# First block of a two-block network on Trainium2: key scores, expert choice, spread and expert sum joined into one stage per layer, with the scores of all experts kept in DRAM

## What is computed

```python
def block(hb):                                   # lax.map over blocks of 128 tokens
    q = (hb @ w_q).reshape(n, PEER_HEADS, 2, PEER_DK_HALF)          # 8 heads, 2 halves of 128
    s = jnp.einsum('nhpk,pek->nhpe', q, keys)                       # 128 keys a half
    v_top, i_top = lax.top_k(s, PEER_TOPK)                          # 16
    cand = (v_top[:, :, 0, :, None] + v_top[:, :, 1, None, :]).reshape(...)
    sc, pos = lax.top_k(cand, PEER_TOPK)
    e = i1 * N_KEYS + i2                                            # of 16384 experts
    g = jax.nn.softmax(sc.astype(jnp.float32), axis=-1)
    a = jax.nn.gelu(jnp.einsum('nhkd,nd->nhk', u_tab[e], hb)) * g
    return jnp.einsum('nhk,nhkd->nd', a, v_tab[e])
x = x + mod[5] * _peer(h, *peer_args)
```

## Time and profile before

| what | us |
|---|---|
| median of 3 runs | 5837.4 |
| lowest and highest | 5792.01 and 5842.43 |
| the profiled execution | 5842.43 |
| its span, first to last instruction | 5842.2 |

### The profile page before, as it was taken

One profiled execution on the slowest core, in us unless ns is written; L12 is line 12 of the kernel. 1 busy time (PEld: TensorE's weight loads), 2 busy tenths in 40 slices (PEclk: granted clock), 3 DMA queues, 4 the chain that ended last, 5 costly groups with the idle time before them and its releaser, 6 DMA issues. The chain is left out here.

```text
span 5842.2 us, 68094 instructions
## 1 busy us (share of the span) xinstructions
PE 4566.9 (78%) x24318; PEld 3796.7 (65%) x24318; DVE 3182.0 (54%) x4967; ACT 1507.1 (26%) x1871; POOL 1088.4 (19%) x304
## 2 busy tenths in 40 slices
PE   6747968766999999999447745999996666985678
PEld 1635735255888888888336635888886666974477
DVE  1533327895555555555354297888886343631455
ACT  0211212132222222222212213333333312531333
POOL 0300011264222221221210135333330010000000
PEclk9857989888999999999767868999998787995689
DMA  6202212334333333332213304555554103541154
GB/s 247 66 19 63 81 66 87 138 136 162 125 109 124 126 117 116 126 124 84 102 33 99 119 29 172 184 185 188 187 192 132 45 26 91 164 129 53 49 143 137
DMA packets 545188, 668.47 MB, mean 114 GB/s; under 512 B 15866, under 2 KB 467482, under 8 KB 543182
## 3 DMA queue, kind: packets, MB, share of 16 engines
q1 hardware_dynamic: 543236, 659.80, 33.7%
q10 hardware_dynamic: 1776, 6.34, 0.3%
HBM read 613.04 MB, written 53.05 MB: 114 GB/s over the span
## 5 line engine op out<-in xcount | busy, mean ns | idle before, releaser
L1320 POOL TENSOR_TENSOR ex_ulo<-ex_u,ex_uhi 128x2048 fp32r<-128x2048 f32 x128 | 595.2, 4650 | 1579.3 <-ACT ex_uhi L1354 1579.3
L119 PE MATMUL bank<-hThi_l,ex_uhi 128*128 128x512 f32 (+1 forms) x2048 | 690.1, 337 | 52.2 <-POOL ex_ulo L1320 52.2
L119 PE MATMUL bank<-hTlo_l,ex_uhi 128*128 128x512 f32 (+1 forms) x2048 | 689.8, 337 | 0.0
L119 PE MATMUL bank<-hThi_l,ex_ulo 128*128 128x512 f32 (+1 forms) x2048 | 689.7, 337 | 0.0
L119 PE MATMUL bank<-ex_vhi,ex_ahi 128*128 128x512 f32 x1536 | 607.6, 396 | 53.6 <-DVE peer_l L1394 50.8
L1394 DVE TENSOR_TENSOR peer_l<-peer_l,bank 128x512 f32<-128x512 f32 x756 | 496.9, 685 | 239.6 <-PE bank L119 239.6
L119 PE MATMUL bank<-ex_vlo,ex_ahi 128*128 128x512 f32 x1536 | 603.9, 393 | 0.0
L119 PE MATMUL bank<-ex_vhi,ex_alo 128*128 128x512 f32 x1536 | 603.7, 393 | 0.0
L1372 DVE TENSOR_TENSOR ex_vlo<-ex_v,ex_vhi 128x2048 fp32r<-128x2048 f32 x128 | 385.7, 3013 | 279.4 <-ACT ex_vhi L1360 279.4
L119 PEld LDWEIGHTS bank<-hThi_l,ex_uhi 128*128 128x128 f32 x2048 | 390.0, 190 | 95.4 <-POOL ex_ulo L1320 52.9
L119 PEld LDWEIGHTS bank<-hTlo_l,ex_uhi 128*128 128x128 f32 x2048 | 390.0, 190 | 42.6
(11 more groups left out here) (476 smaller groups left out, 9305.9 us busy)
## 6 DMA issues: line engine op xcount, KB each, us to landing
ex_u<-peer_u_in SPq DMA_DIRECT2D x128, 1024.0 KB, 8.3
ex_v<-peer_v_in SPq DMA_DIRECT2D x128, 1024.0 KB, 5.4
dense_weights<-sp_buf SPq DMA_DIRECT2D x12, 4096.0 KB
gu_w<-ffn_w_up_in SPq DMA_DIRECT2D x88, 512.0 KB, 5.2
mg_wg<-w_in_in SPq DMA_DIRECT2D x32, 1024.0 KB, 5.3
ex_g<-dense_weights SPq DMA_DIRECT2D x64, 512.0 KB, 4.5
ada_w<-w_ada_in SPq DMA_DIRECT2D x12, 2048.0 KB, 8.2
pc_ada_w<-w_ada_in SPq DMA_DIRECT2D x12, 2048.0 KB
```

Of the source, the lines that this page charges most:

```text
L119: ins = pe.matmul(psum, a, b, start=first and i == 0, stop=last and i == len(terms) - 1)
L1320: pool.tensor_tensor(u2[1][:, s, :, :], u[:, s, :, :], u2[0][:, s, :, :].bitcast(F32), ALU.subtract).then_inc(u_lo, 1)
```

## The change

The four stages become one, `peer`, of which all steps are written out (no hardware loop). It has two phases.

Score phase: 72 steps of the same form, 8 of query weights and 64 of u, n = 0 to 71. ACT splits the high half of step n+1 ahead of taking the results of n, POOL the low half of n+1 ahead of weighing the groups of n. The raw tile and its low half now lie in the same memory, so a tile's slot is free only when its products are done (`scored`, later `used`); there are three slots of tiles in layer 0 and four in layer 1 (`ring`), and three of high halves. The gelus of all experts are written to `act_s` (three slots) and stored by SP in DRAM (`expert_scores`). Beside these steps DVE does the choice of the first pair of tiles and then the second; PE turns the picks after u step 9 and 16 (layer 1: 14), then spreads two groups per step for 32 steps (layer 1: one group per step for 32 steps), and from u step 52 on the 12 chunks of the next modulation, one per step.

Value phase: 64 steps. SP loads the stored scores s and the dense weights g of step m (`fetch_weighted`), then v of step m+3 (m+4 in layer 1). DVE multiplies both experts' columns in one operation, splits v, and makes the low half of a after ACT's high half. PE's `combine(m)` adds all 64 steps into the eight PSUM banks (four in layer 1), so DVE's additions are gone, and at the end each bank is multiplied by the gate and added to x. u and the query weights are laid out on the host so that each partition's part of a tile is one run of 8 KB.

```diff
-def key_scores(K, l, hT, t0, top, topi):
...
-def expert_choice(K, l, top, topi, tiles, choice):
...
+def peer(K, l, hT, x, t0):
...
+    U = NEXP // width
+    first_v = PH + U
+    ring = 3 if tw > 256 else 4
+    slots = 3
+    G = 8
+    n_groups = tw // G
+    per_step = 2 if tw > 256 else 1
+    turn_at = [9, 16] if pairs == 2 else [14]
+    spread_from = turn_at[-1] + 1
+    spread_to = spread_from + n_groups // per_step
+    ada_from = spread_to + 3
+    n_ada = 6 * D // 512 if nxt else 0
...
+        raw = ExitStack()
+        wt = sb("w", [P, ring, KD, width], scope=raw)
+        raw.close()
+        w_lo = sb("wlo", [P, ring, KD, width], F32R)
+        w_hi = sb("whi", [P, slots, KD, width], F32R)
+        act_s = sb("s", [P, 3, 2, tw])
...
+            def _(sp):
+                def fetch(n):
+                    if n >= ring:
+                        if n - ring < first_v:
+                            sp.wait_ge(scored, 2 * (n - ring) + 2)
+                        else:
+                            sp.wait_ge(used, n - ring - first_v + 1)
+                    if n < PH:
+                        src = K.dram["peer_w_q"][l, n]
+                    elif n < first_v:
+                        src = K.dram["peer_u"][l, n - PH]
+                    else:
+                        m = n - first_v
+                        sp.dma_start(wt[:, n % ring, :, :].rearrange("p (e j) c -> p e (j c)", e=2),
+                                     K.dram["peer_v"][l][m * width:(m + 1) * width, :].rearrange("(e p) d -> p e d", p=P)).then_inc(w_in[n % ring], 16)
...
+                def keep_scores(m):
+                    sp.wait_ge(freed, 2 * (PH + m) + 2)
+                    sp.dma_start(K.scores[m, :, 0:2 * tw], act_s[:, m % 3, :, :].rearrange("p e t -> p (e t)")).then_inc(s_stored[m % 3], 16)
+
+                def keep_choice(b):
+                    sp.wait_ge(copied, 16 * (b + 1))
+                    sp.dma_start(K.dense[b], buf[:, b % 2, :, :].rearrange("p i t -> p (i t)")).then_inc(g_stored[b % 2], 16)
+
+                def fetch_weighted(m):
+                    if m >= 3:
+                        sp.wait_ge(mulled, m - 2)
+                    sp.dma_start(act_s[:, m % 3, :, :].rearrange("p e t -> p (e t)"), K.scores[m, :, 0:2 * tw]).then_inc(sg_in[m % 3], 16)
+                    sp.dma_start(gw[:, m % 3, :, :], K.dense[0:nb, :, m * 128:(m + 1) * 128].rearrange("b j n -> j b n")).then_inc(sg_in[m % 3], 16)
...
+                for n in range(1, first_v + lag - PH):
+                    if n < first_v + ring:
+                        fetch(n)
+                    m = n - lag
+                    if m < 0:
+                        continue
+                    keep_scores(m)
+                    for g in groups_after(m):
...
+                    sp.wait_ge(s_stored[s], 16 * ((U - s + 2) // 3))
+                if nxt:
+                    for s in range(2):
+                        sp.wait_ge(row_stored[s], 16 * (n_ada // 2))
+                for m in range(U):
+                    fetch_weighted(m)
+                    if first_v + m + ring < first_v + U:
+                        fetch(first_v + m + ring)
+                    if m == 4:
+                        for s in range(2):
+                            sp.dma_start(mod5[:, s, :], K.ada[l, s:s + 1, 5 * D:6 * D].broadcast_to([P, D])).then_inc(mod_in, 16)
...
+                def split_lo(n):
+                    s = n % slots
+                    pool.wait_ge(hi_ready, n + 1)
+                    pool.tensor_tensor(w_lo[:, n % ring, :, :], wt[:, n % ring, :, :], w_hi[:, s, :, :].bitcast(F32),
+                                       ALU.subtract).then_inc(lo_ready, 1)
...
+                split_lo(0)
+                for n in range(first_v):
+                    if n + 1 < first_v:
+                        split_lo(n + 1)
+                    for g in groups_after(n - PH):
+                        weigh(g)
...
+                def score(n):
+                    pe.wait_ge(lo_ready, n + 1)
+                    for j in range(2):
+                        i = 2 * n + j
+                        if i >= 4:
+                            pe.wait_ge(freed, i - 3)
...
+                        match_keys(n - 1)
+                    m = n - PH
+                    if m in turn_at:
+                        turn(turn_at.index(m))
+                    for g in groups_after(m):
+                        spread(g)
+                    if ada_after(m) is not None:
+                        ada(ada_after(m))
...
+                def combine(m):
...
+                    pe.wait_ge(v_lo, m + 1)
+                    pe.wait_ge(a_lo, m + 1)
+                    for o in range(outs):
...
+                            last.then_inc(outed, 1)
+                    if m < U - 1:
+                        last.then_inc(used, 1)
+
+                for m in range(U):
+                    combine(m)
...
+                def take_scores(m):
+                    for j in range(2):
+                        i = 2 * (PH + m) + j
+                        act.wait_ge(scored, i + 1)
+                        if m >= 3:
+                            act.wait_ge(s_stored[m % 3], 16 * (m // 3))
+                        act.activation(act_s[:, m % 3, j, :], K.ps[i % 4][:, 0:tw], ACT.Gelu_apprx_tanh).then_inc(freed, 1)
...
+                def split_a(m):
+                    act.wait_ge(mulled, m + 1)
+                    if m >= slots:
+                        act.wait_ge(used, m - slots + 1)
+                    act.activation(a2[0][:, m % slots, :, :], a[:, m % slots, :, :], ACT.Copy).then_inc(a_hi, 1)
...
+                for n in range(first_v):
+                    split_hi(n + 1)
...
+                        take_query(n)
+                    else:
+                        take_scores(m)
+                    if 1 <= n <= PH:
...
+                        take_spread(g)
+                    if ada_after(m) is not None:
+                        take_ada(ada_after(m))
+                split_a(0)
+                for m in range(1, U):
+                    split_hi(first_v + m)
+                    split_a(m)
...
-def spread_choice(K, l, choice, t0, tw):
...
-def experts(K, l, hT, acc, t0, tw):
...
+                def multiply(m):
+                    dve.wait_ge(sg_in[m % 3], 32 * (m // 3 + 1))
+                    if m >= slots:
+                        dve.wait_ge(a_hi, m - slots + 1)
+                    dve.tensor_tensor(a[:, m % slots, :, :].rearrange("p e (b t) -> p e b t", t=64),
+                                      act_s[:, m % 3, :, :].rearrange("p e (b t) -> p e b t", t=64),
+                                      gw[:, m % 3, :, :].rearrange("p b (e t) -> p e b t", t=64), ALU.mult).then_inc(mulled, 1)
...
+                for m in range(U):
+                    multiply(m)
+                    split_v(m)
+                    dve.wait_ge(a_hi, m + 1)
+                    dve.tensor_tensor(a2[1][:, m % slots, :, :], a[:, m % slots, :, :], a2[0][:, m % slots, :, :].bitcast(F32),
+                                      ALU.subtract).then_inc(a_lo, 1)
...
-            experts(K, l, hT, acc, t0, TALL - t0)
-            with stage(K, "step") as (block, step):
...
+        peer(K, l, hT, x, t0)
```

## The result

The changed kernel takes 7255.8 us, the median of 4 runs (7248.2 to 7257.5); the kernel before took 5839.9 beside it. The ratio is 1.243, with a 95% interval of 1.238 to 1.248: slower by 1416 us. The forecast was 7466, in a range of 7130 to 7850. Direction and mechanism came out as forecast; the rise, forecast as 7466 - 5837 = 1629 us, was put 213 us too high.

What follows compares the result with a forecast made beforehand. PE bounds the old expert loop; stages around it are not PE-bound. The profiled 5842.4 us plus 834.9 for layer 0 and 794.0 for layer 1 gave 7471, adjusted to the median as 7466 us; range 7130 to 7850.

Steps and rivals of the forecast that it cites:

- The step that decides: SP's value-phase queue: s and g wait behind v, leaving gaps of 13.6 us in layer 0, 10.9 in layer 1.
- The rows to look for: Value phase: g releases DVE, PE clock about 0.9 or below, v load waits for PE, sums every 27 and 19 us.
- Rival A: SP's value-phase queue: s and g arrive before the sum, so gaps and cold starts go; 5602 us, chance 0.04.
- B (full clock throughout): Value phase: PE keeps full clock through the gaps, 128 x 2.5 us less; 7146 us, chance 0.08.
- C (half clock throughout): Value phase: PE's bursts stay at half clock throughout, 603 us more; 8069 us, chance 0.09.
- the prediction's range: Whole kernel: own case 7200 to 7770 us, errors not all on one side; widened towards two rivals, 7130 to 7850.
- 63 gaps: Value phase, each layer: 64 bursts with 63 gaps; gaps total 856.8 us in layer 0, 686.7 in layer 1.
- The turn: Value phase, layer 0: products 10.88, cold start 2.5 and gap 13.6 us make a period of 27.0 us.
- The transfers: Layer 0's value-phase gap: v, s and g, 2 MB, take 8.3 us, bounds 6.95 to 9.6.
- Layer 0's score part: Layer 0, score phase 1058.5 us plus a handover of 15 to the value phase; 1073.5 us together.
- the wait for the choice: Layer 0's score phase: PE waits 8 us for DVE's choice, slowed by POOL's splits; bounds 0 and 36.
- Layer 1's loop: Layer 1's score phase: 32 spreading steps loop through ACT, POOL and PE, 12.3 us each, 393.6 us; bounds 7.9 and 14.5.

Runs made afterwards that it cites:

- experiment 1: Changed kernel with SP's loads of s and g issued three steps ahead, in front of the waiting v load; 5585.3 us, 0.958 of the kernel before.
- experiments 1 and 2: The second: changed kernel with s and g loaded three steps ahead and POOL weighing groups before splitting; 5478.8 us, 0.942 of the kernel before.
- Experiment 6: Changed kernel plus 44 useless PE products before each sum in layer 1's value phase; 7156.0 us.
- Experiment 7: Changed kernel with only POOL's score-phase order altered: it weighs the groups before splitting the next low part; 7140.0 us.
- experiment 5: Changed kernel plus 36 useless PE products before each sum in layer 1's value phase; 7221.3 us.
- experiment 3: Changed kernel with SP's loads of s and g issued one step ahead, before the v load that waits for the sum; 5870.5 us.
- in after: The changed kernel itself, as measured without any further edit; 7255.8 us.

## Why the prediction was right, and where its sizes were off

**The mechanism.** The step that decides, that the s and g of step m+1 stand behind a load of v that waits for sum m, is shown by experiment 1: the same work with another order loses the whole rise. The rows to look for came: DVE released by g, a clock of 0.75 and 0.69, SP's v load 0.03 us behind the sum, and a sum every 26 and 18 us (forecast 27 and 19). Rival A fell, because the three slots were there but never filled ahead. The rule of the Trainium skill's "DMA: Bandwidth & Descriptors", section "Rules for kernel authors", to issue early and wait late, is obeyed in full by experiments 1 and 2, and the trace agrees with it there (sums 10.88 us apart, clock 1.00). Three slots didn't make a transfer early whose issue stood behind the wait of another one (26.2 us per turn).

**Rivals B and C.** B (full clock throughout) fell with the rows at 2524.33, C (half clock throughout) with the return to 0.23 us between products inside every sum, after some 10 products of 48 in layer 0. Experiment 6 measures the clock's price at 1.9 us per sum in layer 1, and 10.4 products of 0.2 us make 2.1 in layer 0, where the forecast had 2.5 for both.

**Where 220 us of the two regions went**, in the prediction's terms. All of the larger errors lie on the same side, which the prediction's range had ruled out ("they will not all fall on one side"); it held the result all the same.

- *The number of gaps.* The term "63 gaps" was wrong. SP is held only while there is a v load to issue, and the last three (layer 1: four) steps have none. SP's and DVE's rows at the end of layer 0 show it; first SP, where the last v is followed by three pairs without a wait for PE:

```profile
3474.26 0.37 SPq L1058 DMA_DIRECT2D pr_w<-peer_v_in  x1
3474.68 0.47 SPq L1081 DMA_DIRECT2D pr_s<-expert_scores  x1
3475.19 0.43 SPq L1082 DMA_DIRECT2D pr_g<-dense_weights  x1
3475.67 1.62 SPq L1081 DMA_DIRECT2D pr_s<-expert_scores  x1
```

```profile
3482.21 1.23 DVE L1392 TENSOR_TENSOR pr_a<-pr_s,pr_g 128x1024 f32<-128x1024 f32 x1 [20.63 <-DMA pr_g<-dense_weights]
...
3486.69 1.22 DVE L1392 TENSOR_TENSOR pr_a<-pr_s,pr_g 128x1024 f32<-128x1024 f32 x1
```

  There were 61 gaps and 60. The missing two and three, with their cold starts, are 2 x 16.1 + 3 x 13.4 = 72 us. This is the one term that was wrong in kind; the others were missed in size. The order of SP's queue, read to its end, would have told it.
- *The turn.* Layer 0: 26.1 us in the mean against 27.0, over 61 turns 55. In the turn shown the transfers took 7.9 us (forecast 8.3), DVE's chain 4.7 (4.9), and tail and SP 0.2 (0.33: SP issued 0.03 us after the product's end and not 0.17); over the layer some 10.4 products per sum ran at half clock (12.5). Layer 1: 17.9 against 18.84, over 60 turns 55; about 9.5 products at half clock.
- *The transfers.* DMA issues of layer 0's value phase (KB each, median us to landing) are quicker than in the loop before, where v took 6.4. The engines' share is lower too, 0.24 against 0.35; that this is the reason wasn't tested:

```profile
pr_w<-peer_v_in SPq DMA_DIRECT2D x57, 1024.0 KB, 4.9
pr_s<-expert_scores SPq DMA_DIRECT2D x59, 512.0 KB, 5.8
pr_g<-dense_weights SPq DMA_DIRECT2D x59, 512.0 KB, 7.0
```

- *Layer 0's score part*, 23 us less: a step with two groups takes 14.6 us where 15.2 was taken (32 of them, 18 us), the wait for the choice, put at 8, didn't occur, and PE waited 12.2 us before the value phase instead of 15. Against that the twelve chunks of the modulation took 8 us more: they added 8.1 each instead of 7.9, and the first added 13.6, of which PE spent 3.9 waiting for its load.
- *Layer 1's loop*, 11.6 us against 12.3 (32 of them, 23 us). POOL's weighing took 1.90 us; the row used had 2.70, but there DVE's one-hots ran beside it. Experiment 7 shows both ends of it, 1.90 and 2.88. The part as a whole fell by 10 only, since the steps without a group took 7.2 us in the mean: 231 us for the 32, where 214.4 and 3 for the turn were taken. Some of them fall beside DVE's choice, where POOL's splits take up to 6.6 us and PE waits for them by up to 2.9.

The sum of the value parts, 186 of 220 us, is thus 72 for gaps that don't exist, 110 for turns taken too long, and 4 not assigned.

**The choice beside POOL's splits.** DVE's rows in layer 1's choice, and POOL's in the same time:

```profile
4152.32 4.52 DVE L1352 CAST pr_place<-pr_pos 128x256 f32<-128x256 uint32 x1
...
4158.99 8.70 DVE L1362 TENSOR_TENSOR pr_hot<-pr_half,iota 128x4096 f32<-128x4096 f32 x1
...
4152.09 4.60 POOL L1128 TENSOR_TENSOR pr_wlo<-pr_w,pr_whi 128x2048 fp32r<-128x2048 f32 x1 [1.96 <-ACT pr_whi L1248]
...
4158.61 4.80 POOL L1128 TENSOR_TENSOR pr_wlo<-pr_w,pr_whi 128x2048 fp32r<-128x2048 f32 x1 [1.92 <-ACT pr_whi L1248]
```

The cast starts just behind a split of POOL's and ends 0.15 us after it: 4.52 us, as one took in the loop before. The comparison of 4096 columns takes 8.70, about its own 4.43 and the 4.42 that POOL's split still had to run; this is the longest of six, of which the median is 4.76. The searches in the same stretch keep their 0.30 us each. That is what the Trainium skill's "SBUF — State Buffer", section "SBUF: two separate sides", would have, where whichever of the two starts first keeps the shared ports for its whole instruction, and the trace agrees as far as these operations go. In layer 0 PE never waited for the choice (0.8 us for the first group behind it), so neither the 8 us nor the bound of 36 was used.

## What to carry to other kernels

An engine's queue is in order, so a prefetch has the lead that the slowest wait in front of it leaves, not that of its buffers: before joining or reordering stages, write down SP's queue and ask of each wait who stands behind it. Issue first what can go now, and last what needs a slot that PE has still to free; three steps' lead made a loss of 24% into a gain of 4%. And when several engines pass work round, put the short operation that others wait for ahead of the long one that they don't (POOL's weighing: 3 us per step, 100 to 112 us in all).

## What was not expected of the hardware

- A short wait can cost the clock too. After 8.32 us of products and a wait of 1.94 us, products fell to the lower level a microsecond into the sum (the row at 5028.86), and so they did in most of experiment 5's 60 sums, though not in the one before, after 1.96 us. In experiment 3's layer 0 (clock 0.99), where two sums of 10.9 us often ran without a gap before the wait, most waits of 2 us cost nothing (the row at 2023.02). After 4.62 us the first product was already slow. What tells the cases of 2 us apart stays open.
- POOL and DVE take longer when both have work all the time. In experiment 7 POOL's operations grow from 1.90 to 2.88 us and from 4.6 to 5.55, and DVE's one-hots from 1.18 us each (2.36 for two in after, where POOL stands idle meanwhile) to 4.2 in the mean:

```profile
4243.79 25.12 DVE L1385 TENSOR_TENSOR pr_hot<-pr_choice,iota 128x1024 f32<-128x1024 f32 x6
```

  Alone, the four operations of a step would take 1.90 + 4.6 + 2.36 = 8.9 us one after the other; side by side they take 8.4. The two engines together get hardly more done than one after the other would; PE's own work of 7.9 us stands close below.
- More work on PE made the kernel faster: 60 x 44 useless products in gaps brought 112 us (experiment 6). Without gaps, as in experiment 1, PE has clock 1.00 anyway, so there is nothing for them to bring.
